# Order of ScalarE's and VectorE's operations in two attention loops, a later mask load, and an absolute value by masking bits

## The chip, the cores and the metric

The kernel runs on one core of one Trainium2 chip. The metric is device time in microseconds (us) of one execution; the median of three runs is compared. A core has TensorE (PE, matrix products and transposes), VectorE (DVE), ScalarE (ACT), GpSimd (POOL) and SyncE (SP, which here issues all transfers). Each runs its own list of instructions in order, and they meet at semaphores. Matrix products land in PSUM, in eight banks of 128 x 512 float32 (`ps[0]` to `ps[7]`), from which ACT or DVE read them.

## What is computed

Two transformer blocks over 512 tokens of width 1024, in float32. The first has window attention, a long convolution, differential attention, gates and a feed-forward network; the second has forgetting attention and stick-breaking attention (8 heads of 64 each), and a feed-forward network with a short convolution. The change touches two of the attentions:

```python
def diff_attention(q, k, v, lam):                      # first block, 4 heads
    s = einsum('bhcqd,bhckd->bhcqk', q, k) / sqrt(64)  # c = 0, 1
    p = softmax(s)
    a = p[:, :, 0] - lam * p[:, :, 1]
    return einsum('bhqk,bhkd->bhqd', a, v)

def stick_breaking_attention(q, k, v):                 # second block, 8 heads
    z = einsum('bhqd,bhkd->bhqk', q, k) * 64 ** -0.5
    log_beta = log_sigmoid(z)
    log_one_minus = where(mask, log_sigmoid(-z), 0.0)
    after = cumsum(log_one_minus, reverse=True) - log_one_minus
    weights = where(mask, exp(log_beta + after), 0.0)
    return einsum('bhqk,bhkd->bhqd', weights, v)
# the stick output then gets an rms norm over its 512 columns, gain sb_out_g
```

## The kernel before

**Weights.** All weight matrices pass through in 244 slots of at most 128 x 1024. SP loads a slot into one of three `wraw` buffers (line 2278), ACT rounds it to `whi` (L1562), DVE takes the rest `wlo` (L920), and PE multiplies three times (`hi*hi, hi*lo, lo*hi`) for each of the slot's four blocks; a block is six matmuls of 512 columns. ACT and DVE prepare a slot when PE starts the second slot ahead of it. The slots make groups, named after their weights (`sk`, `sv`, `fq`, `fk`, `fv`, ...), and a group's results are read at its last slot (L1450 reads those of `fq` and `fk`, L1187 those of `bA`).

**Attention beside the weights.** Each attention is a generator on every engine, with steps `u = 0, 1, 2, ...`; after a block of weights a group takes a step of it, 1, 2, 3 or 4 to a slot as the group's rate says. So the order on every engine is fixed by where the calls stand in the code. All engines take the same steps at the same blocks, each as far as its waits allow.

**Differential attention**, beside the groups `bA0` to `gC1`. Unit `u` is a query block and a head. PE: `scores(u)` into banks 4 and 5 (it waits until ACT has read them, semaphore `c_ex`), `turn(u - 2)` transposes the combined weights into bank 6 (waits for `c_cb`), `values(u - 3)`. DVE: `highest(u)` takes the maxima of banks 4 and 5 (L1210, L1212), then `combine(u - 1)` subtracts the two softmaxes (L1219 to L1225). ACT: `shares(u)`, the two exponentials (L1739). Every fourth unit the output is normed and turned through bank 6 as well; ACT takes `ochi` (L1756) and DVE `oclo` (L1244) from it, which frees the bank.

**Stick-breaking attention**, beside the groups `sv` (rate 1), `fq` (2), `fk` and `fv` (4). Units 0 to 7 have 512 columns of keys, 8 to 15 have 128, 16 to 23 have 384, 24 to 31 have 256. In step `u`:

- PE: `turn(u - 4)` transposes the sums `Lb` into bank 6, for even `u` `scores(u)` into banks 4 and 5 for two units, `values(u - 5)`.
- ACT: `copy(u)` reads the scores into `zb` (L1872), `logs(u - 1)` makes `log(1 + exp(-|z|))` (L1877, L1879), `weights(u - 4)` reads the turned bank 6 through an exponential (L1887).
- DVE: `sums(u - 2)` is the scan (L1375) and an addition (L1378), `parts(u)` makes `|z|` (L1367) and `min(-z, 0)` (L1368) from `zb`.

The norm of the stick output goes through the last quarter of the same bank 6, one quarter of 128 columns in each of four steps: PE turns it ahead of `turn`, ACT rounds it to `ohi` (L1864), DVE takes the rest `olo` (L1343). PE's next turn, quarter or not, waits until bank 6 has been read: by `weights` (semaphore `s_ev`) and, if there was a quarter, by `olo` (`o_lo`).

**The mask.** `mk` holds the masks of the second block's attentions. SP loads it behind the weights of slot 145, once POOL has finished a norm (`p_acc` at 35), and DVE copies it to `mkR` behind group `sq`, whose slots are 142 to 145.

Of the kernel before, what the change touches and what calls it, by code (L numbers as in the profile page):

```python
# [4 lines left out]

F32 = mybir.dt.float32
F32R = mybir.dt.float32r
ALU = mybir.AluOpType
ACT = mybir.ActivationFunctionType
AX = mybir.AxisListType  # L10
# [152 lines left out]
def build(nc, d, out):  # L163
# [231 lines left out]
    def tensor_program(t):  # L395
# [326 lines left out]
        def out_norm_piece(q, k):  # L722

            w.wait_ge(o_sc, 3 * q + 3)
            across(6, 3, W5[5][:, k * 128:(k + 1) * 128]).then_inc(o_tr, 1)
            return o_lo, 4 * q + k + 1

        def stick():
            w.wait_ge(qk_c, 8)

            def scores(u):

                n, wd = s_units[u][0], 128 * (s_units[u][0] + 1)
                for i in range(2):
                    take(4 + i)
                    base, j = 64 * i, s_units[u][1] // 2
                    mm(ps[4 + i][:, 0:wd], sqT[base:base + 64, j, n * 128:(n + 1) * 128], skT[base:base + 64, j, 0:wd], True, False)
                w.wait_ge(s_mk, 2)
                for i in range(2):
                    mm(ps[4 + i][:, n * 128:wd], identR[:], mkR[:], False, True).then_inc(s_qk, 1)  # L740
                    free[4 + i] = [(s_z, u + i + 1)]

            def turn(u):
                wd = 128 * (s_units[u][0] + 1)
                w.wait_ge(s_sum, u + 1)
                take(6)
                read = [(s_ev, u + 1)]
                if u >= 11 and u % 8 in (3, 4, 5, 6):
                    read.append(out_norm_piece(u // 8 - 1, u % 8 - 3))
                for k in range(wd // 128):  # L750
                    op = across(6, k, Lb[u % 5][:, k * 128:(k + 1) * 128])
                op.then_inc(s_tr, 1)
                free[6] = read

            def values(u):
                n, h = s_units[u]
                w.wait_ge(s_ev, u + 1)
                w.wait_ge(sv_c, n + 1)
                if h == 0:
                    take(7)  # L760
                for k in range(n + 1):
                    op = mm(ps[7][:, h * 64:(h + 1) * 64], PT2[u % 2][:, k * 128:(k + 1) * 128], sv[:, k, h * 64:(h + 1) * 64],
                            k == 0, k == n)
                op.then_inc(s_pv, 1)
                if h == 7:
                    free[7] = [(o_c, u // 8 + 1)]

            for u in range(37):
                if 4 <= u < 36:
                    turn(u - 4)  # L770
                if u < 32 and u % 2 == 0:
                    scores(u)
                if u >= 5:
                    values(u - 5)
                yield
# [135 lines left out]
    def vector_program(v):  # L911
# [290 lines left out]
        def differential():  # L1202
# [43 lines left out]
                                       ALU.subtract).then_inc(oc_lo, 1)  # L1246

            for u in range(22):
                if u < 16:
                    highest(u)  # L1250
                if 1 <= u <= 16:
                    combine(u - 1)
                if u >= 9 and u % 4 == 1:
                    low((u - 9) // 4)
                if u >= 7 and u % 4 == 3:
                    squares((u - 7) // 4)
                if 3 <= u < 19 and (u - 3) % 4 == 3:
                    scaled_out((u - 3) // 4)
                yield
# [100 lines left out]
        def stick():  # L1360
            def parts(u):
                wd = 128 * (s_units[u][0] + 1)
                z, L, nr = zb[u % 3], Lb[u % 5], W5[u % 3]
                w.wait_ge(s_z, u + 1)
                if u >= 5:
                    w.wait_ge(s_tr, u - 4)
                v.scalar_tensor_tensor(L[:, 0:wd], z[:, 0:wd], -1.0, z[:, 0:wd], ALU.mult, ALU.max).then_inc(s_ab, 1)  # L1367
                v.tensor_scalar(nr[:, 0:wd], z[:, 0:wd], -1.0, 0.0, ALU.mult, ALU.min).then_inc(s_ab, 1)  # L1368

            def sums(u):  # L1370
# [9 lines left out]
            for u in range(37):  # L1380
                if 2 <= u < 34:
                    sums(u - 2)
                if u < 32:
                    parts(u)
                if 15 <= u < 35 and u % 8 in (7, 0, 1, 2):
                    out_norm_piece((u - 15) // 8, (u - 15) % 8)
                yield

        fox_go = []
# [161 lines left out]
    def scalar_program(a):  # L1551
# [314 lines left out]
        def stick():  # L1866
# [20 lines left out]
                a.activation(PT2[u % 2][:, 0:wd], ps[6][:, 0:wd], ACT.Exp).then_inc(s_ev, 1)  # L1887

            for u in range(37):
                if u < 32:  # L1890
                    copy(u)
                if 1 <= u <= 32:
                    logs(u - 1)
                if 4 <= u < 36:
                    weights(u - 4)
                if 15 <= u < 35 and u % 8 in (7, 0, 1, 2):
                    out_norm_piece((u - 15) // 8, (u - 15) % 8)
                if u >= 5 and (u - 5) % 8 == 7:
                    q = (u - 5) // 8
                    w.wait_ge(s_pv, u - 4)  # L1900
# [369 lines left out]
    def sync_program(s):  # L2270
# [32 lines left out]
        weights(24, 66)  # L2303
        w.wait_ge(c_qk, 32)
        s.dma_start(x[:], x_dram).then_inc(in_res, 16)
        weights(66, 146)
        w.wait_ge(p_acc, 35)
        s.dma_start(mk[:], d["mask2"]).then_inc(in_mask, 16)
        weights(146, 158)
        w.wait_ge(fl_v, 5)  # L2310
        s.dma_start(f_dram, W5[5][0:8, :]).then_inc(fl_d, 16)
        w.wait_ge(fl_d, 16)
# [166 lines left out]
```

## Time and profile before

| | us |
|---|---|
| median of 3 runs (lowest, highest) | 1635.25 (1634.95, 1635.26) |
| the profiled execution, its time | 1634.98 |
| its span, first to last instruction | 1633.2 |
| PE busy | 1610.7, 99% of the span |
| DVE busy | 885.2, 54% |
| ACT busy | 636.1, 39% |
| POOL busy | 238.5, 15% |
| mean granted clock of PE | 0.999 |

Times in the trace count from the start of the span. The differential attention lies at about 442 to 533 us, the stick-breaking attention at about 1037 to 1162 us. PE's rows overlap: a matmul of 512 columns is drawn 0.39 us long, and the next starts 0.23 us after it, so PE can stand still for 0.16 us before a row shows a gap.

### The profile page before, as it was taken

What the parts mean: (1) busy time and instruction counts of PE and PEld (TensorE: products, weight loads), DVE (VectorE), ACT (ScalarE), POOL (GpSimd) and SP (SyncE); (2) the same over time, 40 slices, a digit from 0 to 9 for tenths busy, and PEclk for the clock granted to TensorE, in tenths of its full rate; (3) what the DMA queues carried; (4) which work ended last, traced back from release to release, by engine and by line L of the source; (5) the groups of instructions that cost most, each with busy time, mean ns of one, the idle gap of its engine ahead of it and who ended that gap; (6) DMA issues with size and microseconds to landing.
All of it is one profiled execution on the core that took longest, in us unless ns stands there. A gap on an engine that the chain in (4) does not pass through costs nothing.

```text
span 1633.2 us, 19219 instructions
## 1 busy us (share of the span) xinstructions
PE 1610.7 (99%) x7584; PEld 1275.3 (78%) x7584; DVE 885.2 (54%) x1447; ACT 636.1 (39%) x1089; POOL 238.5 (15%) x216
## 2 busy tenths in 40 slices
PE   7999999999999999999999999999999999999998
PEld 5667788876767888888888888786788888888887
DVE  6556456755477455433333324578555677777322
ACT  4332124456445433322322222456563344434222
POOL 1323303400031134111000203000013200000000
PEclk9999999999999999999999999999999999999999
DMA  7121113221111333233323322421103332322322
GB/s 276 42 77 40 52 57 104 90 78 52 66 52 59 122 92 95 89 99 103 99 95 99 96 90 73 168 65 39 53 3 102 92 101 87 95 91 90 129 91 77
DMA packets 39733, 142.12 MB, mean 87 GB/s; under 512 B 4531, under 2 KB 5299, under 8 KB 39260
## 3 DMA queue, kind: packets, MB, share of 16 engines
q1 hardware_dynamic: 39644, 140.89, 26.7%
q8 instruction: 60, 0.98, 0.3%
q14 instruction: 29, 0.24, 0.0%
HBM read 138.76 MB, written 2.11 MB: 86 GB/s over the span
## 4 chain that ended last, share of the span: by engine, by line
PE 91%; POOL 3%; DVE 2%; ACT 1%; issue 1%; DMA 0%; SPq 0%; POOLq 0%; ACTq 0%; DVEq 0%
PE ps L406 87%; PE ps L409 3%; POOL sqs L2151 2%; POOL sqt L2149 1%; DVE wlo L920 0%; ACT whi L1562 0%; DMA x<-in_x 0%; PE ps L906 0%; ACT PT L1887 0%; ACT zb L1872 0%; DVE W L1375 0%; ACT Lb L1877 0%; DVE tp L1120 0%; ACT tp L1685 0%; DVE st L1107 0%
## 5 line engine op out<-in xcount | busy, mean ns | idle before, releaser
L920 DVE TENSOR_TENSOR wlo<-wraw,whi 128x1024 fp32r<-128x1024 f32 (+2 forms) x244 | 304.2, 1251 | 448.9 <-ACT whi L1562 448.4
L406 PE MATMUL ps<-hThi,whi 128*128 128x512 f32 x1128 | 455.9, 404 | 0.0
L1562 ACT ACTIVATE whi<-wraw 128x1024 fp32r<-128x1024 f32 (+2 forms) x244 | 252.1, 1037 | 484.5 <-PE ps L406 454.6
L406 PE MATMUL ps<-hThi,wlo 128*128 128x512 f32 x1128 | 440.4, 390 | 0.0
L406 PE MATMUL ps<-hTlo,whi 128*128 128x512 f32 x1128 | 440.0, 390 | 0.0
L406 PEld LDWEIGHTS ps<-hThi,whi 128*128 128x128 f32 x1128 | 212.3, 188 | 59.7 <-issue 19.1
L406 PEld LDWEIGHTS ps<-hThi,wlo 128*128 128x128 f32 x1128 | 212.1, 188 | 45.5
L406 PEld LDWEIGHTS ps<-hTlo,whi 128*128 128x128 f32 x1128 | 212.5, 188 | 44.5 <-issue 3.6
L406 PE MATMUL ps<-whi,hThi 128*128 128x512 f32 (+1 forms) x224 | 87.0, 388 | 0.4 <-ACT rk L1679 0.4
L406 PE MATMUL ps<-whi,hTlo 128*128 128x512 f32 (+1 forms) x224 | 84.2, 376 | 0.0
L406 PE MATMUL ps<-wlo,hThi 128*128 128x512 f32 (+1 forms) x224 | 83.9, 375 | 0.0
L406 PE MATMUL ps<-whi,achi 128*128 128x512 f32 x176 | 69.2, 393 | 0.0
L406 PE MATMUL ps<-whi,aclo 128*128 128x512 f32 x176 | 68.6, 390 | 0.0
L406 PE MATMUL ps<-wlo,achi 128*128 128x512 f32 x176 | 68.5, 389 | 0.0
L406 PE MATMUL ps<-achi,whi 128*128 128x512 f32 x176 | 68.5, 389 | 0.0
L406 PE MATMUL ps<-aclo,whi 128*128 128x512 f32 x176 | 68.5, 389 | 0.0
L406 PE MATMUL ps<-achi,wlo 128*128 128x512 f32 x176 | 68.5, 389 | 0.0
L2168 POOL TENSOR_TENSOR ft<-ft,R 128x512 f32<-128x512 f32 x22 | 27.9, 1290 | 199.1 <-ACT ft L1806 199.1
L1817 ACT ACTIVATE ft<-vt,vec 128x512 f32<-128x512 f32 x44 | 34.8, 813 | 51.1 <-DVE vt L1312 51.1
L2265 POOL TENSOR_TENSOR small<-small,vec 128x1 f32<-128x1 f32 x4 | 2.2, 541 | 349.1 <-DVE small L1537 349.1
L406 PEld LDWEIGHTS ps<-whi,hThi 128*128 128x128 f32 x224 | 42.2, 189 | 10.4 <-issue 2.9
L406 PEld LDWEIGHTS ps<-whi,hTlo 128*128 128x128 f32 x224 | 42.2, 188 | 7.9
(310 smaller groups left out, 2429.8 us busy)
## 6 DMA issues: line engine op xcount, KB each, us to landing
wraw<-in_ws SPq DMA_DIRECT2D x236, 512.0 KB, 3.5
x<-in_x SPq DMA_DIRECT2D x4, 512.0 KB, 5.7
x<-in_x SPq DMA_DIRECT2D x1, 2048.0 KB, 9.9
Fb<-forget_rows SPq DMA_DIRECT2D x1, 2048.0 KB, 8.5
out<-ys SPq DMA_DIRECT2D x8, 256.0 KB, 2.4
w<-in_w SPq DMA_DIRECT2D x2, 512.0 KB, 12.3
dec<-in_dec SPq DMA_DIRECT2D x1, 1024.0 KB, 14.9
wraw<-in_ws SPq DMA_DIRECT2D x4, 256.0 KB, 2.6
```

Of the source, the lines that this page charges most:

```text
L406: return t.matmul(o, l, r, start=first, stop=last)
L409: return t.transpose(ps[b][:, c * 128:(c + 1) * 128], src, ident)
L920: v.tensor_tensor(wlo[h][:, 0:width(i)], wraw[h][:, 0:width(i)], whi[h][:, 0:width(i)].bitcast(F32), ALU.subtract).then_inc(lo_done[h], 1)
L1562: a.activation(whi[h][:, 0:width(i)], wraw[h][:, 0:width(i)], ACT.Copy).then_inc(hi_done[h], 1)
L1817: a.activation(ft[i][:], vt[q % 4][:], ACT.Identity, bias=col("cb2", c), scale=col("cw2", 88 + c)).then_inc(v_a, 1)
L2149: g.tensor_tensor(sqt[:], xT[:, f, :], xT[:, f, :], ALU.mult).then_inc(p_acc, 1)
L2151: g.tensor_tensor(sqs[:], sqs[:], sqt[:], ALU.add).then_inc(p_acc, 1)
L2168: g.tensor_tensor(t[:], t[:], R1[:], ALU.mult).then_inc(u_sr, 1)
L2265: g.tensor_tensor(small[:, 8 + b:9 + b], small[:, 4 + b:5 + b], col("mhalf"), ALU.pow).then_inc(w_r, 1)
```

## The change

Five edits. No instruction is added or taken away except that one operation on DVE is exchanged for another.

1. Differential attention, DVE: `combine(u - 1)` is issued before `highest(u)`.
2. Stick-breaking attention, ACT: `weights(u - 4)` first, then the quarter, then `copy(u)` and `logs(u - 1)`.
3. Stick-breaking attention, DVE: the quarter after the sums and before `parts(u)`. The quarters run one step later on all three engines (steps 16 to 19, 24 to 27 and 32 to 35; before 15 to 18, 23 to 26, 31 to 34).
4. `|z|` is made by clearing the sign bit of an integer view, a `tensor_scalar`, in place of a `scalar_tensor_tensor` that takes `max(-z, z)`.
5. SP loads the mask behind slot 148 in place of slot 145.

```diff
@@ PE, stick, turn(u)
-                if u >= 11 and u % 8 in (3, 4, 5, 6):
-                    read.append(out_norm_piece(u // 8 - 1, u % 8 - 3))
+                if u >= 12 and u % 8 > 3:
+                    read.append(out_norm_piece(u // 8 - 1, u % 8 - 4))
@@ DVE, differential
             for u in range(22):
+                if 1 <= u <= 16:
+                    combine(u - 1)
                 if u < 16:
                     highest(u)
-                if 1 <= u <= 16:
-                    combine(u - 1)
@@ DVE, stick, parts(u)
-                v.scalar_tensor_tensor(L[:, 0:wd], z[:, 0:wd], -1.0, z[:, 0:wd], ALU.mult, ALU.max).then_inc(s_ab, 1)
+                v.tensor_scalar(L[:, 0:wd].bitcast(I32), z[:, 0:wd].bitcast(I32), 0x7FFFFFFF, None, ALU.bitwise_and).then_inc(s_ab, 1)
@@ DVE, stick
                 if 2 <= u < 34:
                     sums(u - 2)
+                if 16 <= u < 36 and u % 8 < 4:
+                    out_norm_piece(u // 8 - 2, u % 8)
                 if u < 32:
                     parts(u)
-                if 15 <= u < 35 and u % 8 in (7, 0, 1, 2):
-                    out_norm_piece((u - 15) // 8, (u - 15) % 8)
@@ ACT, stick
             for u in range(37):
+                if 4 <= u < 36:
+                    weights(u - 4)
+                if 16 <= u < 36 and u % 8 < 4:
+                    out_norm_piece(u // 8 - 2, u % 8)
                 if u < 32:
                     copy(u)
                 if 1 <= u <= 32:
                     logs(u - 1)
-                if 4 <= u < 36:
-                    weights(u - 4)
-                if 15 <= u < 35 and u % 8 in (7, 0, 1, 2):
-                    out_norm_piece((u - 15) // 8, (u - 15) % 8)
@@ SP
-        weights(66, 146)
+        weights(66, 149)
         w.wait_ge(p_acc, 35)
         s.dma_start(mk[:], d["mask2"]).then_inc(in_mask, 16)
-        weights(146, 158)
+        weights(149, 158)
```

The order of VectorE's instructions in steps 2 and 3 of the differential attention before (the two gate operations stand at the head of each step, `Pc_142` is unit 1):

```order
L1187 SCALAR_TENSOR_TENSOR gate_109<-gate_109,ps 128x512 x2
L1210 TENSOR_REDUCE st<-ps 128x1
L1212 TENSOR_SCALAR st<-st 128x1
L1210 TENSOR_REDUCE st<-ps 128x1
L1212 TENSOR_SCALAR st<-st 128x1
L1219 RECIPROCAL st<-st 128x1
L1221 SCALAR_TENSOR_TENSOR st<-st,small 128x1
L1223 RECIPROCAL st<-st 128x1
L1225 SCALAR_TENSOR_TENSOR Pc_142<-Pc_143,st,Pc_142 128x512
```

The same step of VectorE after the change (its lines are numbered one higher):

```order
L1188 SCALAR_TENSOR_TENSOR gate_109<-gate_109,ps 128x512 x2
L1220 RECIPROCAL st<-st 128x1
L1222 SCALAR_TENSOR_TENSOR st<-st,small 128x1
L1224 RECIPROCAL st<-st 128x1
L1226 SCALAR_TENSOR_TENSOR Pc_142<-Pc_143,st,Pc_142 128x512
L1211 TENSOR_REDUCE st<-ps 128x1
L1213 TENSOR_SCALAR st<-st 128x1
```

The combination of unit 1 has moved ahead of the maxima of unit 2.

ScalarE's instructions in stick steps 23 and 24 before, around the rounding of a weight slot (`zb_207` is the copy of unit 23, `PT_1_195` the turned bank of unit 19, `ohi` the quarter):

```order
L1872 ACTIVATE zb_207<-ps 128x384
L1877 ACTIVATE Lb_202<-Lb_202 128x384
L1879 ACTIVATE Lb_202<-Lb_202,vec 128x384
L1887 ACTIVATE PT_1_195<-ps 128x384
L1864 ACTIVATE ohi<-ps,vec 128x128
L1562 ACTIVATE whi_56<-wraw_53 128x1024
L1872 ACTIVATE zb_205<-ps 128x256
L1877 ACTIVATE Lb_203<-Lb_203 128x384
L1879 ACTIVATE Lb_203<-Lb_203,vec 128x384
L1887 ACTIVATE PT_0_194<-ps 128x384
```

The same place on ScalarE after the change:

```order
L1888 ACTIVATE PT_1_195<-ps 128x384
L1873 ACTIVATE zb_207<-ps 128x384
L1878 ACTIVATE Lb_202<-Lb_202 128x384
L1880 ACTIVATE Lb_202<-Lb_202,vec 128x384
L1563 ACTIVATE whi_56<-wraw_53 128x1024
L1888 ACTIVATE PT_0_194<-ps 128x384
L1865 ACTIVATE ohi<-ps,vec 128x128
L1873 ACTIVATE zb_205<-ps 128x256
```

The reading of the turned bank now heads each step, the quarter has gone from step 23 to step 24, and the slot's rounding keeps its place at the step's end.

VectorE in the same stretch before, from the first sum of step 24 on (`Kf` reads a result of group `fk`, `olo` is a quarter):

```order
L920 TENSOR_TENSOR wlo_59<-wraw_53,whi_56 128x1024
L1450 SCALAR_TENSOR_TENSOR Kf<-ps,R_160 128x512
L1375 SCALAR_TENSOR_TENSOR W_1_189<-W_1_189,Lb_202 128x384
L1378 TENSOR_TENSOR Lb_202<-zb_206,W_1_189 128x384
L1367 SCALAR_TENSOR_TENSOR Lb_204<-zb_205 128x256
L1368 TENSOR_SCALAR W_0_188<-zb_205 128x256
L1343 SCALAR_TENSOR_TENSOR olo<-ps,vec,ohi 128x128
```

And VectorE there after the change:

```order
L921 TENSOR_TENSOR wlo_59<-wraw_53,whi_56 128x1024
L1451 SCALAR_TENSOR_TENSOR Kf<-ps,R_160 128x512
L1376 SCALAR_TENSOR_TENSOR W_1_189<-W_1_189,Lb_202 128x384
L1379 TENSOR_TENSOR Lb_202<-zb_206,W_1_189 128x384
L1344 SCALAR_TENSOR_TENSOR olo<-ps,vec,ohi 128x128
L1368 TENSOR_SCALAR Lb_204<-zb_205 128x256
L1369 TENSOR_SCALAR W_0_188<-zb_205 128x256
```

The quarter is two operations nearer to the head of the step, but still behind the slot's rest, the reading of `Kf` and the sums; the absolute value has become a `TENSOR_SCALAR`.

## Rows read from the trace of the kernel before

**Rows 1.** Waits of PE: engine, line and tile, waited for, total us, times, longest.

```profile
PE ps L409 <- DVE olo L1343: 3.0, 6, 0.9
PE ps L409 <- DVE Pc L1225: 1.5, 1, 1.5
...
PE ps L409 <- ACT PT L1887: 0.7, 2, 0.3
```

**Rows 2.** Timeline, 452 to 457 us: start, length, engine, line, operation, [idle before].

```profile
452.82 0.68 DVE L1210 TENSOR_REDUCE st<-ps 128x1 f32<-128x512 f32 x1
...
453.73 0.69 ACT L1739 ACTIVATE Pc<-ps,st 128x512 f32<-128x512 f32 x1 [1.49 <-DVE st L1212]
...
454.39 0.15 DVE L1219 RECIPROCAL st<-st 128x1 f32<-128x1 f32 x1
...
455.04 0.75 DVE L1225 SCALAR_TENSOR_TENSOR Pc<-Pc,st,Pc 128x512 f32<-128x512 f32 x1
...
455.85 0.65 PE L409 MATMUL ps<-vec,Pc 128*128 128x128 f32 x4 [1.48 <-DVE Pc L1225]
456.43 1.13 PE L406 MATMUL ps<-kcT,qcT 64*128 64x512 f32 x4
```

**Rows 3.** Timeline, 492 to 494 us, where a normed output frees bank 6.

```profile
492.73 0.75 DVE L1244 SCALAR_TENSOR_TENSOR oclo<-ps,vec,ochi 128x512 fp32r<-128x512 f32 x1 [0.24 <-ACT ochi L1756]
...
493.69 0.49 PE L409 MATMUL ps<-vec,Pc 128*128 128x128 f32 x3
```

**Rows 4.** Timeline, 1105 to 1108 us, stick steps 16 and 17.

```profile
1105.14 0.49 ACT L1872 ACTIVATE zb<-ps 128x384 f32<-128x384 f32 x1 [1.45 <-PE ps L406]
...
1106.26 0.39 PE L406 MATMUL ps<-hTlo,whi 128*128 128x512 f32 x1
...
1106.49 0.39 PE L406 MATMUL ps<-hThi,wlo 128*128 128x512 f32 x1
...
1106.72 0.35 DVE L1343 SCALAR_TENSOR_TENSOR olo<-ps,vec,ohi 128x128 fp32r<-128x128 f32 x1 [0.23 <-ACT ohi L1864]
...
1107.22 0.30 PE L409 MATMUL ps<-vec,W 128*128 128x128 f32 x1 [0.34 <-DVE olo L1343]
```

**Rows 5.** Timeline, 1125 to 1133 us, stick steps 23 to 25.

```profile
1125.14 0.48 ACT L1872 ACTIVATE zb<-ps 128x384 f32<-128x384 f32 x1
...
1125.47 0.49 PE L409 MATMUL ps<-vec,Lb 128*128 128x128 f32 x3
...
1126.95 0.36 ACT L1864 ACTIVATE ohi<-ps,vec 128x128 fp32r<-128x128 f32 x1
...
1127.20 1.06 ACT L1562 ACTIVATE whi<-wraw 128x1024 fp32r<-128x1024 f32 x1
...
1132.03 0.35 DVE L1343 SCALAR_TENSOR_TENSOR olo<-ps,vec,ohi 128x128 fp32r<-128x128 f32 x1
...
1132.52 0.30 PE L409 MATMUL ps<-vec,W 128*128 128x128 f32 x1 [0.94 <-DVE olo L1343]
```

**Rows 6.** Timeline, 1150 to 1156 us, stick steps 31 to 33.

```profile
1150.05 0.37 ACT L1872 ACTIVATE zb<-ps 128x256 f32<-128x256 f32 x1
...
1150.56 0.38 PE L409 MATMUL ps<-vec,Lb 128*128 128x128 f32 x2
...
1155.47 0.30 PE L409 MATMUL ps<-vec,W 128*128 128x128 f32 x1 [0.52 <-DVE olo L1343]
```

**Rows 7.** VectorE's groups by form, 1000 to 1170 us: count, busy us, mean ns, idle before.

```profile
L1367 DVE SCALAR_TENSOR_TENSOR Lb<-zb 128x384 f32<-128x384 f32 x8 | 4.4, 555 | 1.6 <-ACT zb L1872 1.6
...
L1368 DVE TENSOR_SCALAR W<-zb 128x384 f32<-128x384 f32 x8 | 2.8, 353 | 0.0
```

**Rows 8.** The mask's tile: duration ns min/median/max, first and last start us.

```profile
L2308 SPq DMA_DIRECT2D mk<-in_mask x1: 328/328/328, 995.0 to 995.0; - x1
L1509 DVE CAST mkR<-mk x1: 219/219/219, 1006.0 to 1006.0; 128x128 fp32r<-128x128 f32 x1
...
DMA to landing us min/median/max: 2.9/2.9/2.9
```

More of the change, by code:

```diff
@@ L7 @@
 F32R = mybir.dt.float32r
+I32 = mybir.dt.int32
 ALU = mybir.AluOpType
```

## The prediction

> **What bounds the kernel now.** PE is busy for 99% of the span, so I read first what it waits for. Most of the list lies at the start of the program or in norms that the change doesn't touch. Three entries lie in the two attentions: `olo` 3.0 us in 6 waits, `PT` (`weights`) 0.7 us in 2, and `Pc` (`combine`) 1.5 us in one [rows 1]. The reader should see what is not in the list: PE never waits for the sums `Lb` of the stick attention, only for its bank 6 to be read.
>
> A gap in a row is shorter than what PE loses. Two matmuls start 0.23 us apart (1106.26, 1106.49), but each is drawn 0.39 us long [rows 4]. So 0.16 us is to be added to each gap: the turn at 1107.22 was due at 1106.72 and lost 0.50 us, where its row says 0.34. In this measure the eight stick waits cost 3.7 + 8 x 0.16 = 5.0 us, the differential one 1.48 + 0.16 = 1.64 us. The change can win 6.6 us, 0.4% of 1635, and no more.
>
> **The change, part by part.**
>
> *Differential, removed.* PE's turn of unit 1 starts at 455.85 and was due at 454.21. DVE comes to this step at 452.82, and does the maxima of unit 2 first; the combination runs from 454.39 to 455.79, 1.40 us [rows 2]. In the new order the combination runs from 452.82 to 454.22, and the turn starts at 454.28. That wins 1.57 us.
>
> *Differential, what is late next.* The maxima of unit 2 now start at 454.14, 1.32 us later. ACT's first exponential starts 0.91 us after them (452.82 to 453.73) [rows 2], so at 455.05, and is done with its sum some 0.77 us later, at 455.82; the second ends at 456.6. Behind the turn on PE stands `scores(3)`, which needs banks 4 and 5. It follows the turn by 0.58 us (455.85 to 456.43), so it is due at 454.86, waits until 455.87 for bank 4, and its second half until 456.67 for bank 5. It ends at 457.2; before, at 456.43 + 1.06 = 457.49. Of 1.57 us 0.3 is left. Six steps on, the maxima still come some 0.3 us late, as DVE meets a weight slot first and then does the combination ahead of them, and behind them stands the normed output: `oclo` ends at 493.48 and PE turns at 493.69, 0.21 us later, of which some 0.15 is the way from DVE to PE (1107.07 to 1107.22) [rows 3, 4]. This loses 0.2. Sum: 0.1 us won.
>
> *Stick, a wait that goes.* At step 16 ACT stands idle for 1.45 us before `copy(16)` at 1105.14, for scores that PE makes behind its turn, and reads the turned bank only after that. With `weights` first, the reading and the quarter's `ohi` (0.36 us) [rows 5] fit into the idle time. DVE's `olo` at 1106.72 stood idle for its `ohi` [rows 4], and now also has the two `parts` operations behind it (0.555 + 0.353 us) [rows 7]: it starts at 1105.8, is done at 1106.2, and PE's turn, due at 1106.72, doesn't wait. The 0.50 us go. Of the eight waits the two large ones below (1.10 and 0.68) are left to tell; the five others have 5.0 - 0.50 - 1.78 = 2.7 us. I moved the rows in the same way through those steps, each operation to the later of its engine and its input: two were waits for `weights` behind two logarithms, which it now leads, and go; the three others go where DVE is through with its sums in time. I am left with 0.3 us in two of them, where DVE isn't; 2.4 us go.
>
> *Stick, two waits that stay.* At step 25 PE waits until 1132.52, 0.94 + 0.16 = 1.10 us, for an `olo` that starts at 1132.03 [rows 5]. In front of it DVE has a slot's rest `wlo`, one `Kf` and the sums, and `wlo` begins when ACT's `whi` is done. That begins later now: before, ACT did `copy(23)` at 1125.14 without waiting for the turn of step 23, and reached `whi` 2.06 us later, with `weights` and a quarter (0.25 us, 1126.95 to 1127.20) between. Now step 23 opens with a wait for the turn, which ends at 1125.47 + 0.49 = 1125.96; the same operations without the quarter are 1.81 us, and `whi` begins at 1127.8, 0.6 us later. DVE has the two `parts` less in front of `olo`, 0.91 us at 384 columns [rows 7] and about two thirds of it at the 256 here, so 0.6. The two cancel, and the wait stays at 1.1 us. At step 33 the pattern returns: the turn of step 31 ends at 1150.94, `copy(31)` had begun at 1150.05 [rows 6], and now comes after the turn and 0.27 us of `weights`, at 1151.2. Without the quarter `whi` is 0.65 late; here DVE had no `parts` to put behind `olo` (steps 32 and on have none), so the whole 0.65 reaches PE: 0.52 + 0.16 becomes 1.3 us.
>
> *Sum for the stick attention:* 5.0 before; left are 0.3 + 1.1 + 1.3 = 2.7. Won 2.3, between 0 (all waits come back behind slots) and 5.0 (none does).
>
> *The absolute value.* The trace shows no integer operation on DVE. Bounds are the same tile's two forms at 384 columns: 555 ns as it is, 353 ns as the `TENSOR_SCALAR` beside it [rows 7]. I take 353, as it is the nearest in form. DVE then has 0.2 us a step less, 5 us over 32 units, but all of it behind `olo`, and PE waits for no sum. At either end it is worth 0; a way for it to lose would be a form slower than 555, which the same argument hides.
>
> A page speaks against this edit: the Trainium skill, "SBUF — State Buffer" (Who interferes with whom), has a VectorE operation at its two-port double rate and a GpSimd operation block each other for their whole length. No run here shows it; GpSimd has three operations per norm in this stage, the last of which is needed for a quarter that now comes a step later than before, so by that rule the sum would stay as it is. By the Trainium skill, "VectorE: DVE Perf Modes" (What auto-detection actually checks), the double rate is open to one source in SBUF as far as the firmware enables it for the operation; by that the new form is at either bound, and the sum the same.
>
> *The mask.* SP's load goes out at 995.0 and lands 2.9 us later; DVE copies it at 1006.0 [rows 8]. The load still waits for the same norm, and slots 146 to 148 go out ahead of it instead of standing behind. Lost only if it came 8 us later; PE shows no wait here, so nothing is won either. 0 us; the cover is those 8 us.
>
> **Sum.** 0.1 + 2.3 = 2.4 us. The profiled execution took 1634.98 us with a span of 1633.2, 0.27 us below the median; from the median, 1635.25 - 2.4 = 1632.9, or 0.14%. A measurement of this kernel can tell 0.2%, 3.3 us, from no change.
>
> **The rivals.**
>
> *A. As above, the waits move behind the slots.* 1631.9 to 1634.2. Chance 0.54.
>
> *B. The gain comes whole.* The bank is read right behind the turn, and DVE reaches `olo` in time also at slots: 5.0 us in the stick attention, 0 to 1.6 in the other, 1630.2 down to 1628.6. It needs `whi` at steps 23 and 31 no later than before. For it: 8 of 8 stick waits are of the kind that the new order aims at. Against it: at 1132.03 `olo` has no idle time in its row, so its `ohi` was there, and DVE itself was late [rows 5]. With partial forms (one of the two waits gone) everything below 1632.0: chance 0.25.
>
> *C. Nothing is won.* A second wait of the kind of the one for bank 4 (1.0 us) stands at a later gate step of the differential attention, and in the stick attention two more slot starts have their `whi` 0.65 us late. 2.4 - 1.0 - 1.3 leaves 0.1 us: 1635.2, with 1634.2 to 1636.5 around it. For it: DVE meets a slot's rest or gates ahead of the combination in every second step. Against it: at those steps the second exponential ends, by the same reckoning, before its bank is due. Chance 0.17.
>
> *D. Slower.* ACT is in order, and each odd step's `copy`, which needed no new scores, now stands behind the turn: 1.2 us later at steps 23 and 31. If the sums were due that tightly, PE would wait 1.2 us at each of the ten odd steps from 13 to 31: 12 us, less the 5.0, gives 1642. It decides from the point where a sum is ready less than 1.2 us ahead of its turn. Against it: no wait for a sum in the list [rows 1]. Chance 0.04.
>
> **How the numbers follow.** The likeliest is A, 1632.9. From 1630.2 to 1636.0 takes in most of B's whole stick gain and nearly all of C, leaving out D and B's end with both gains, some 0.15. A alone has 1631.9 to 1634.2. Faster by over 0.2% is below 1631.98: B, and a little of A's edge, 0.27. Slower by over 0.2% is above 1638.5: D and a rest, 0.05. Within: 0.68.
>
> **What would show it.** In the new trace PE should have no wait for `Pc`, but one of some 1 us for ACT's reading of banks 4 and 5 ahead of `scores(3)`, near 455. The `olo` waits should be fewer, the two large ones near 1130 and 1153, each with a `wlo` just before its `olo`; no `PT` wait. The new absolute value should show 353 ns at 384 columns. The forecast is wrong if either of those two waits is under 0.5 us, if a wait for `Lb` appears, or if `whi` of step 23 starts no later against its turn than before.

## The result, and the profile after

The changed kernel takes 1639.88 us (median of 15 runs) against 1635.25 us before (15 runs). The ratio of the means, 1.0024 with a 95% interval of 1.0017 to 1.0030, says 0.24% slower, where 1632.9 us had been forecast. One execution of each kernel here, two of e10 and one of e11 were over 10% longer than the others; ranges and ratios leave them out, medians count them. The profiled execution took 1639.91 us with a span of 1638.1, 4.9 us more than before.

I laid each PE instruction of one trace beside the same one of the other and read how much later it starts. This shift is -0.4 us at 450 us. Between 455 and 489 us it grows by 7.4, to 7.0 us. It stays there to 1100, past the mask's place, and falls by 2.2 to 2.4 us in the stick attention. So the forecast failed in the differential attention alone.

PE's waits, to be laid beside [rows 1] (lines are numbered one higher now):

```profile
PE ps L410 <- DVE olo L1344: 2.3, 2, 1.2
PE ps L407 <- ACT Pc L1740: 1.9, 3, 0.9
PE ps L410 <- DVE Pc L1226: 1.2, 1, 1.2
```

The wait for `Pc` was to go and is still there. The waits for ScalarE's reading of banks 4 and 5 (`ACT Pc`) are three, not one. Only the two for `olo` are as forecast. The timeline at the first gate step answers to [rows 2]:

```profile
452.08 2.53 POOL L2118 TENSOR_TENSOR merged<-merged,gate 128x512 f32<-128x512 f32 x2 [134.25 <-DVE gate L1188]
...
452.51 0.16 DVE L1220 RECIPROCAL st<-st 128x1 f32<-128x1 f32 x1
...
452.70 0.69 DVE L1222 SCALAR_TENSOR_TENSOR st<-st,small 128x1 f32<-128x1 f32 x1
...
453.31 0.15 DVE L1224 RECIPROCAL st<-st 128x1 f32<-128x1 f32 x1
...
453.50 1.66 DVE L1226 SCALAR_TENSOR_TENSOR Pc<-Pc,st,Pc 128x512 f32<-128x512 f32 x1
...
455.21 0.66 PE L410 MATMUL ps<-vec,Pc 128*128 128x128 f32 x4 [1.15 <-DVE Pc L1226]
...
456.81 2.07 PE L407 MATMUL ps<-kcT,qcT 64*128 64x512 f32 x3 [0.94 <-ACT Pc L1740]
```

Two operations of the combination are longer: L1222 takes 0.69 us and L1226 1.66, where a step without a gate shows 0.22 and 0.75:

```profile
465.17 0.22 DVE L1222 SCALAR_TENSOR_TENSOR st<-st,small 128x1 f32<-128x1 f32 x1
...
465.50 0.75 DVE L1226 SCALAR_TENSOR_TENSOR Pc<-Pc,st,Pc 128x512 f32<-128x512 f32 x1
```

The combination lasts from 452.51 to 455.16, 2.65 us and not 1.40. The GpSimd row is the one to look at: it adds the branch to `merged`, two additions back to back until 454.61. L1222 ends when the first addition does (452.08 + 1.26 = 453.34, by half of the row), and L1226 ends 0.55 us after the second. GpSimd isn't slowed, 2.53 us for two as before. In the trace of before these additions ran from 452.39 to 454.92, beside the maxima, which showed their usual 0.68 [rows 2], and reached only the first of the combination's two operations:

```profile
452.39 2.53 POOL L2117 TENSOR_TENSOR merged<-merged,gate 128x512 f32<-128x512 f32 x2 [134.26 <-DVE gate L1187]
...
454.58 0.34 DVE L1221 SCALAR_TENSOR_TENSOR st<-st,small 128x1 f32<-128x1 f32 x1
```

In the changed kernel the next three combinations at gate steps read the same: 0.66 and 1.65 us at 458.06 and 458.82, 0.67 and 1.67 at 478.14 and 478.91, 0.66 and 1.66 at 484.06 and 484.83, each with two additions beside them.

PE's granted clock, in windows over the same place (columns: window, its length, busy us and number of instructions of PE, of its weight loads, DVE, ACT and POOL, the granted clock, then DMA):

```profile
440.00:455.00 15.00, 14.06 (x60) 8.80 (x58) 10.38 (x20) 5.13 (x11) 2.53 (x2) 1.00 0.23 70
455.00:460.00 5.00, 3.85 (x10) 1.82 (x11) 4.86 (x11) 2.05 (x5) 2.49 (x2) 0.65 0.00 0
460.00:465.00 5.00, 5.00 (x20) 4.31 (x20) 3.14 (x7) 2.50 (x5) 0.00 (x0) 0.67 0.00 0
465.00:500.00 35.00, 34.04 (x171) 23.88 (x170) 25.94 (x58) 15.79 (x35) 8.31 (x8) 1.00 0.16 46
```

PE lost 1.31 us in the first wait and 1.01 in the second, which ends at 456.81. The clock falls to the lower level of 1.2 GHz within the second wait, at 456.5, and is back at 2.4 at 463.3. Before, it stood at 1.00 through this stage. In these 6.8 us matmuls start 0.43 us apart:

```profile
461.89 0.63 PE L407 MATMUL ps<-oalo,whi 128*128 128x512 f32 x1
462.32 0.63 PE L407 MATMUL ps<-oahi,wlo 128*128 128x512 f32 x1
462.75 0.63 PE L407 MATMUL ps<-oahi,whi 128*128 128x512 f32 x1
```

By their mean granted clocks not every execution has the fall. Nine of the fourteen of ordinary length have 0.997 or 0.998 and took 1639.1 to 1641.5 us. The other five have 0.999 or 1.0 and took 1636.4 to 1638.2, still more than any of the kernel before (1634.3 to 1636.1).

Three later steps wait for scores, at 482.24, 488.36 and 494.80, since their maxima came late:

```profile
482.24 1.91 PE L407 MATMUL ps<-kcT,qcT 64*128 64x512 f32 x4 [0.50 <-ACT Pc L1740]
488.36 1.69 PE L407 MATMUL ps<-kcT,qcT 64*128 64x512 f32 x4
494.80 1.91 PE L407 MATMUL ps<-kcT,qcT 64*128 64x512 f32 x4 [0.46 <-ACT Pc L1740]
```

Four score matmuls undisturbed take 1.13 us [rows 2]. The shift grows by 3.2 us over these three places. The first two stand behind the combinations of the gate steps at 478 and 484. The third stands behind one without additions of gates. There GpSimd multiplies `ocs` for the norm, and L1222 stands beside it in the same way:

```profile
491.19 1.09 DVE L1222 SCALAR_TENSOR_TENSOR st<-st,small 128x1 f32<-128x1 f32 x1
...
491.23 1.04 POOL L2130 TENSOR_TENSOR ocs<-ocs,st 128x512 f32<-128x512 f32 x1
```

Before, that multiplication lay beside the maxima (485.17 to 486.21), and L1221 took 0.22.

The stick attention answers to [rows 5, 6]. At step 25:

```profile
1133.68 1.23 DVE L921 TENSOR_TENSOR wlo<-wraw,whi 128x1024 fp32r<-128x1024 f32 x1 [1.38 <-ACT whi L1563]
...
1134.83 0.69 DVE L1451 SCALAR_TENSOR_TENSOR Kf<-ps,R 128x512 f32<-128x512 f32 x1
...
1135.43 0.95 DVE L1376 TENSOR_TENSOR_SCAN W<-W,Lb 128x384 f32<-128x384 f32 x1
1136.41 0.56 DVE L1379 TENSOR_TENSOR Lb<-zb,W 128x384 f32<-128x384 f32 x1
1136.89 0.35 DVE L1344 SCALAR_TENSOR_TENSOR olo<-ps,vec,ohi 128x128 fp32r<-128x128 f32 x1
...
1137.38 0.30 PE L410 MATMUL ps<-vec,W 128*128 128x128 f32 x1 [1.05 <-DVE olo L1344]
```

`olo` stands behind the slot's rest, `Kf` and the sums, and PE loses 1.21 us (0.16 more than its row says, as before); at step 33, near 1160, it loses 1.37. Of the other six of eight waits four are gone, two are down to 0.2 us. ScalarE's `whi` of step 23 starts 2.37 us after the step's turn, where it was 1.73 before: 0.6 later, as forecast. The new absolute value takes what the operation beside it takes [rows 7]:

```profile
L1368 DVE TENSOR_SCALAR Lb<-zb 128x384 int32<-128x384 int32 x8 | 2.8, 354 | 0.3 <-ACT zb L1873 0.2
L1369 DVE TENSOR_SCALAR W<-zb 128x384 f32<-128x384 f32 x8 | 2.8, 353 | 0.0
```

### The profile page after: what moved, and what is told of

The parts are those of the page before. It is cut to its first block, busy times and chain, and to the rows that moved or that the text cites. A ratio compares the mean times of both kernels' runs of the same rounds, so it can differ in the third digit from the quotient of the medians.

```text
span 1638.1 us, 19219 instructions
## 1 busy us (share of the span) xinstructions
PE 1615.5 (99%) x7584; PEld 1278.8 (78%) x7584; DVE 887.2 (54%) x1447; ACT 638.2 (39%) x1089; POOL 240.3 (15%) x216
## 4 chain that ended last, share of the span: by engine, by line
PE 90%; POOL 3%; DVE 3%; ACT 1%; issue 1%; DMA 0%; SPq 0%; POOLq 0%; ACTq 0%; DVEq 0%
PE ps L407 87%; PE ps L410 3%; POOL sqs L2152 2%; POOL sqt L2150 1%; ACT whi L1563 0%; DVE wlo L921 0%; DVE Pc L1226 0%; ACT Pc L1740 0%; DVE st L1211 0%; DMA x<-in_x 0%; DVE gate L1188 0%; PE ps L907 0%; DVE st L1222 0%; POOL small L2044 0%; DVE tp L1121 0%
```

## The experiments

There were three rounds of timing, each beside the kernel before on the same chip, and a last one of single profiles. The rounds' medians of the kernel before differ by 0.5 us, so each row is to be read against its own. The theory, P: VectorE's operations that read SBUF twice stand still while GpSimd adds, this makes the combination 1.25 us longer at gate steps, and from it come the waits and the fall of the clock. The rival, Q: the new order of VectorE's queue does it by itself.

| kernel | us, median (lowest to highest) | before | ratio, 95% |
|---|---|---|---|
| e1 stick edits, no differential edit | 1632.44 (1631.42 to 1632.96) | 1635.39 | 0.9981 (0.9973 to 0.9990) |
| e2 differential edit alone | 1642.99 (1639.96 to 1643.76) | 1635.39 | 1.0041 (1.0028 to 1.0053) |
| e3 as e2, additions of one column | 1635.25 (1634.88 to 1636.41) | 1635.39 | 1.0000 (0.9992 to 1.0009) |
| e4 before, additions of one column | 1634.90 (1633.72 to 1636.67) | 1635.39 | 0.9999 (0.9990 to 1.0008) |
| e5 as e1, quarter ahead of the sums | 1630.19 (1629.09 to 1631.54) | 1634.93 | 0.9968 (0.9956 to 0.9980) |
| e6 stick order alone | 1632.85 (1632.53 to 1635.03) | 1634.93 | 0.9989 (0.9980 to 0.9998) |
| e7 old order, late additions | 1642.57 (1642.03 to 1643.56) | 1634.93 | 1.0048 (1.0036 to 1.0061) |
| e8 new order, late additions | 1633.41 (1632.36 to 1635.74) | 1634.93 | 0.9991 (0.9982 to 1.0000) |
| e9 as e5, combination in the middle | 1629.76 (1628.99 to 1630.31) | 1635.06 | 0.9968 (0.9955 to 0.9980) |
| e10 changed, first additions late | 1637.79 (1635.46 to 1639.36) | 1635.06 | 1.0014 (1.0004 to 1.0023) |
| e11 changed, one tensor input | 1638.80 (1635.04 to 1640.73) | 1635.06 | 1.0017 (1.0008 to 1.0026) |
| e12 stick order on ScalarE alone | 1634.69 (1633.83 to 1635.11) | 1635.06 | 0.9998 (0.9989 to 1.0007) |

**e1.** The edit, in the changed kernel:

```diff
             for u in range(22):
-                if 1 <= u <= 16:
-                    combine(u - 1)
                 if u < 16:
                     highest(u)
+                if 1 <= u <= 16:
+                    combine(u - 1)
```

> The changed kernel with one edit undone: in the differential attention VectorE does highest(u) ahead of combine(u - 1) again. Theory P (the combination beside GpSimd's gate additions is what failed; the other edits did as forecast): the trace shows the stick attention's loss of PE time down by 2.2 us (7.02 to 4.81 in the shift of the changed kernel), and nothing lost elsewhere, so 1635.25 - 2.2 = 1633.0 us, between 1632.6 and 1633.5, and the granted clock of PE never falls near 456 us. Rival R (part of the 7 us comes from the other edits, the mask's or the quarters', which only shows together): 1634 or more.

Measured: 1632.44, 0.2 under the range. The shift against before falls by 2.2 us in the stick attention, and there is no other loss. This is as P has it.

**e2.** The same lines changed the other way, in the kernel before.

> The kernel before with one edit: combine(u - 1) ahead of highest(u) in the differential attention. Theory P: everything that was lost comes from here, 7.4 us of which some 3.5 is PE's granted clock falling to half for 6.8 us, so 1642.4 us with the fall and 1638.5 to 1640 without it; VectorE's L1221 and L1225 show 0.69 and 1.66 us at the four gate steps in place of 0.22 and 0.75. Rival R: under 1637, the rest of the loss needs the other edits.

Measured: 1642.99. The five executions are of two kinds: 1639.96 and 1640.73 with a mean granted clock of 0.999, and 1642.99 to 1643.76 with 0.997. The profiled one, which shows no fall of the clock, is of the first kind, and its shift grows by 5.15 us in the differential attention, against 7.4 in the changed kernel's trace with the fall. Its waits:

```profile
PE ps L406 <- ACT Pc L1739: 1.9, 3, 0.9
PE ps L409 <- DVE Pc L1225: 1.2, 1, 1.2
```

They are the same as in the changed kernel. So the fall costs 2.3 us in the traces, 2.8 between the two kinds (1640.35 to 1643.14, their medians) and 3.2 between those of the changed kernel (1636.78 to 1639.94). It comes in some executions and not in others, at the same waits. Why stays open.

**e3 and e4.** On GpSimd:

```diff
+                if j == 1:
+                    m, gt = m[:, 0:1], gt[:, 0:1]
                 g.tensor_tensor(m, m, gt, ALU.add).then_inc(b_p, 1)
```

> As the one before, but GpSimd's eight additions merged + gate of the second branch (those that lie in the first steps of the differential attention) are done over one column of 512, the rest is left out; the order of all engines and every semaphore stay. Theory P (VectorE's two operations with two inputs in SBUF stand while GpSimd reads SBUF): L1221 and L1225 show 0.22 and 0.75 us at all four gate steps, the combination takes 1.40 us, PE's turn(1) doesn't wait, scores(3) waits about 1.0 us, the four later steps have their maxima 1.25 us earlier and wait under 0.2 us each, the clock stays at full speed: within 1 us of the kernel before, 1634.9 to 1636.2. Rival Q (the order of VectorE's queue alone does it, the additions are no matter): as the one before, within 0.5 us.

> The kernel before with the same eight additions cut to one column (the rest of the sum is left out), as a control. In the old order only L1221 lies beside GpSimd's additions, at steps 2 and 6: 0.34 should become 0.22 and the wait of turn(1) 0.1 us shorter. Both theories: within 0.3 us of the kernel before.

Both kernels leave out the rest of the sum. Measured: 1635.25 and 1634.90, not to be told from the kernel before (e4 is 0.5 us below it, where 0.3 at most was expected). In e4 the turn waits 1.52 us in place of 1.64, as expected. In e3 the combination of the first gate step is short again, with the order of e2:

```profile
451.82 0.15 DVE L1219 RECIPROCAL st<-st 128x1 f32<-128x1 f32 x1
452.01 0.22 DVE L1221 SCALAR_TENSOR_TENSOR st<-st,small 128x1 f32<-128x1 f32 x1
452.15 0.16 DVE L1223 RECIPROCAL st<-st 128x1 f32<-128x1 f32 x1
452.34 0.75 DVE L1225 SCALAR_TENSOR_TENSOR Pc<-Pc,st,Pc 128x512 f32<-128x512 f32 x1
```

The only wait left in the list from the differential attention is the one forecast for `scores(3)`:

```profile
PE ps L406 <- ACT Pc L1739: 0.9, 1, 0.9
```

The shift of e3 grows by 0.55 us over the stage, and 4.6 of the 5.15 us of e2 come with the additions. Q is out. Of the 0.55 us, 0.1 is lost at the first gate step. The rest goes at one place, where bank 5 is read late, and ahead of it stands GpSimd's multiplication of `ocs`, which this edit does not touch:

```profile
483.67 1.09 DVE L1221 SCALAR_TENSOR_TENSOR st<-st,small 128x1 f32<-128x1 f32 x1
483.70 1.04 POOL L2131 TENSOR_TENSOR ocs<-ocs,st 128x512 f32<-128x512 f32 x1
...
487.56 1.62 PE L406 MATMUL ps<-kcT,qcT 64*128 64x512 f32 x4
```

L1221 is 0.87 us longer there than elsewhere, and the four matmuls 0.49 longer than undisturbed. So the order by itself may cost 0.1 us only; no run moves the multiplication away. The cut additions also make GpSimd's work shorter, which is why two tests with whole additions follow.

**e7.** The converse: the old order, with GpSimd's additions moved beside the combination.

```diff
+                if j == 1 and k % 2 == 0:
+                    w.wait_ge(c_mx, (12, 16, 28, 32)[k // 2])
                 g.tensor_tensor(m, m, gt, ALU.add).then_inc(b_p, 1)
```

> The converse test: the order of before everywhere, but GpSimd's gate additions of the four gate steps wait until the maxima of that step are done, so that they lie beside the combination, which stands behind the maxima. Nothing is left out. Theory P (two-input operations of VectorE stand while GpSimd adds): L1221 and L1225 take 0.7 to 1.1 and 1.66 us at these four steps, the combination ends 1.3 to 1.8 us later, PE's turn(1) waits 2.9 to 3.4 us in place of 1.63, turns 2, 5 and 6 wait 0.6 to 1.2 us each; the sum is 3.7 to 5.5 us over the kernel before, and some 3.4 more in executions in which PE's clock falls: 1639 to 1644. Rival Q (the place of the maxima matters, not the additions): nothing on VectorE changes, 1635.3 within 0.5.

Measured: 1642.57, 7.6 us slower, with VectorE's and PE's order untouched.

```profile
453.94 1.32 DVE L1221 SCALAR_TENSOR_TENSOR st<-st,small 128x1 f32<-128x1 f32 x1
...
453.98 2.48 POOL L2119 TENSOR_TENSOR merged<-merged,gate 128x512 f32<-128x512 f32 x2 [136.49 <-DVE st L1212]
...
455.37 1.64 DVE L1225 SCALAR_TENSOR_TENSOR Pc<-Pc,st,Pc 128x512 f32<-128x512 f32 x1
...
457.07 1.11 PE L409 MATMUL ps<-vec,Pc 128*128 128x128 f32 x4 [3.34 <-DVE Pc L1225]
```

The combination now ends at 457.0, and PE's wait is 3.34 + 0.16 = 3.5 us, a little over the range. Turn 2 had no wait of its own; turns 5 and 6 had 1.7 and 1.3, more than the 0.6 to 1.2 expected. The clock fell in this trace too (0.61 granted from 455 to 460 us), at 455.9, within the long wait. P's mechanism holds, and the time is in its range; its single waits were put somewhat low.

**e8.** The changed kernel, with the additions waiting for the combination (`c_cb` at 8, 12, 24, 28 in place of `c_mx`).

> The changed kernel, in which GpSimd's gate additions wait until the step's combination is done, so that they lie beside the maxima, whose inputs are in PSUM. Nothing is left out. Theory P: combinations of 1.40 us, turn(1) without a wait, scores(3) waits 1.0 us for ScalarE's reading of banks 4 and 5 and the clock stays at full speed; the differential attention costs as much as before (as with additions of one column), the stick attention wins its 2.2: 1632.4 us, within 0.6. Rival U (additions beside the maxima, or beside the next gate operation, hold up VectorE as well): 1634 to 1640.

Measured: 1633.41, with everything computed, against 1639.88 for the changed kernel in another round. That is 0.4 over P's range and 0.6 under U's. In the trace the differential attention costs 0.6 us more than before, where P had nothing, with L1222 at 1.09 us beside the `ocs` multiplication as in e3, and the stick attention wins its 2.2. GpSimd's additions (454.04 to 456.54) lie beside the maxima and the next gate operations, and neither is longer:

```profile
454.60 0.68 DVE L1211 TENSOR_REDUCE st<-ps 128x1 f32<-128x512 f32 x1
...
455.40 1.28 DVE L1188 SCALAR_TENSOR_TENSOR gate<-gate,ps 128x512 f32<-128x512 f32 x2
```

The gate operation has two inputs as well, but one of them in PSUM.

**e11.** What in the operation makes it stand? In the changed kernel:

```diff
-                v.scalar_tensor_tensor(P0[:], P1[:], st[:, o + 4:o + 5], P0[:], ALU.mult, ALU.add).then_inc(c_cb, 1)
+                v.tensor_scalar(P0[:], P1[:], st[:, o + 4:o + 5], None, ALU.mult).then_inc(c_cb, 1)
```

> The changed kernel, with the last operation of the combination cut to one tensor input: Pc[1] times the factor, without the addition of Pc[0] (that sum is left out). GpSimd's additions stay beside it. If only VectorE's operations with two tensors in SBUF stand, this one takes what such an operation takes elsewhere, 0.42 us for 512 columns, at all four gate steps, while L1222 keeps its 0.67; the combination ends 1.2 us earlier, and the time is 1634.5 to 1636.5. If any read of SBUF by VectorE stands beside GpSimd's additions, it takes 1.2 to 1.6 us there, and 0.42 at the undisturbed steps, and the time is 1638 to 1641.

Measured: 1638.80, and at a gate step and at one without gates:

```profile
453.09 1.40 DVE L1226 TENSOR_SCALAR Pc<-Pc,st 128x512 f32<-128x512 f32 x1
...
464.56 0.49 DVE L1226 TENSOR_SCALAR Pc<-Pc,st 128x512 f32<-128x512 f32 x1
```

The rows decide for the second alternative: this operation with one tensor input takes 1.39 to 1.41 us at all four gate steps and 0.49 elsewhere, so two inputs are not what it needs to stand. The time by itself would not tell: of nine executions five have the lower clock of 0.997 and took 1638.5 to 1640.7, four have 0.999 or 1.0 and took 1635.0 to 1636.6. The time of a `TENSOR_SCALAR` grows by 0.52 ns for each column (L1369 of the changed kernel: 221 ns at 128 columns, 420 at 512), that of the two-input `TENSOR_TENSOR` L1379 by 1.04 (293 and 692 ns). So it reads about two columns in a nanosecond, and it stands all the same. The Trainium skill, "SBUF — State Buffer" (Who interferes with whom), names both kinds: a VectorE instruction with two inputs in SBUF against a GpSimd one that reads SBUF, and one at its two-port double rate; whichever comes second is blocked for the other's whole length, and `tensor_reduce` is free of it. The traces agree. Beside GpSimd's additions an operation with two inputs takes 1.66 us (the changed kernel) and 1.64 (e7), one with a single input at the faster rate 1.40 (e11), and `TENSOR_REDUCE` its usual 0.68 (e8). Away from them the first takes 0.75 (e3, e8) and the second 0.49.

**e10.** Only the first pair of additions waits (`if j == 1 and k == 0: w.wait_ge(c_cb, 8)`).

> The changed kernel, in which only the first two of GpSimd's gate additions (first gate step) wait for the combination; at the other three gate steps they lie beside it as in the changed kernel. It parts the first contention and the fall of PE's clock from the later waits. Theory: turn(1) doesn't wait, scores(3) waits 1.0 us, the clock doesn't fall in any execution, and so 3 us go as well; the later waits of scores at steps 6 to 9 stay, 2.5 to 3.3 us. So between the kernel with all additions late (1633.41) and the changed one (1639.88): 1635.9 to 1636.9, with no execution over 1638. Rival: the clock falls all the same behind the waits of 478 to 495 us, in some executions, and these are 3 us longer.

Measured: 1637.79, over the range. The profiled execution has 1635.66, no wait of a turn for `Pc`, a shift that grows by 4.1 us over the stage, and a clock of 1.00 all along. But of its nine comparable executions two stand at 1639.28 and 1639.36, and four show a clock of 0.998. The part "no execution over 1638" failed. Whether it was by the rival's fall of the clock, no trace shows.

Three more profiles were to show where the clock falls then:

> The kernel with the first two additions late once more, for one profile. Of its nine comparable executions four stood at 1635.5 to 1636.4 with a granted clock of 0.999 to 1.0 and five at 1637.4 to 1639.4 with 0.998 or 0.999; the profiled one had no fall. Theory: where the clock falls, it falls right behind a wait of scores near 480, 486 or 492 us, and matmuls start 0.43 us apart for some microseconds. Rival: it falls elsewhere, in a place that has nothing to do with these waits.

> The same kernel and the same expectation, for a second profile, since the fall comes in about half of its executions.

> The same kernel and the same expectation, for a third profile.

Measured: 1636.07, 1636.51 and 1637.79, with clocks of 1.0, 0.999 and 1.0. In none of them did it fall in the attentions, nor anywhere else before the last 4 us. Where it falls in the slower executions of e10, if it does, stays open. The three also differ by 1.7 us in their times. That difference arises at the very start: PE's first matmul waits for `x` until 8.31, 7.60 and 9.49 us, and at 20 us the shifts against the kernel before are -0.8, -0.5 and 1.0. Executions of this kernel differ by such an amount without any fall.

**e6.** The new order of the stick attention without the new absolute value and the later mask.

> Only the new order in the stick attention, on ScalarE, VectorE and TensorE: no new absolute value, no later mask, the old order in the differential attention. By the forecast the absolute value and the mask are worth 0: same as the kernel with them, 1632.4, within 0.4 us. Rival: the 0.2 us a step less on VectorE (0.553 to 0.354 us at 384 columns) matter at the two slot steps where VectorE is late, up to 0.4 us each, so 1632.8 to 1633.3.

Measured: 1632.85. Against its own kernel before it wins 2.1 us, where e1 won 2.9, but the two intervals overlap, and by time alone the rival is not out. The traces say more: the shift falls by 2.1 us here and 2.2 in e1, and the two large waits are 1.20 and 1.38 us here and 1.20 and 1.36 in e1. Absolute value and mask are worth 0.1 us there, not to be told from nothing.

**e12.** As e1, with VectorE's quarter behind `parts(u)`, as it was before.

> The kernel with the differential order undone (1632.44), with VectorE's quarter behind parts(u) as before and the quarters at the new steps: the new order of the stick attention on ScalarE alone. It parts the 2.2 to 2.5 us won between the two engines. By the reckoning in the prediction, olo comes 0.55 to 0.9 us later wherever there are parts ahead of it: the wait at step 25 grows from 1.20 to 1.8 us, the one at step 33 stays 1.37, step 16 and the like have 0.5 us to spare: 1633.0 to 1634.0. Rival: VectorE's move is worth nothing, 1632.4, or all of it, 1634.9.

Measured: 1634.69, and a shift of -0.75 at 1102 us and -0.74 at 1155. ScalarE's order alone wins nothing; the rival "all of it" is right. VectorE's move alone was not run. The two large waits are 1.60 and 1.37 us, where 1.8 and 1.37 were expected, but new ones come at steps that were thought to have time, as here, where `olo` was ready in every respect but VectorE's queue:

```profile
1113.32 0.35 DVE L1368 TENSOR_SCALAR Lb<-zb 128x384 int32<-128x384 int32 x1
1113.59 0.35 DVE L1369 TENSOR_SCALAR W<-zb 128x384 f32<-128x384 f32 x1
1113.86 0.34 DVE L1344 SCALAR_TENSOR_TENSOR olo<-ps,vec,ohi 128x128 fp32r<-128x128 f32 x1
...
1114.35 0.52 PE L410 MATMUL ps<-vec,Lb 128*128 128x128 f32 x3 [0.56 <-DVE olo L1344]
```

**e5.** As e1, with the quarter moved once more:

```diff
-                if 2 <= u < 34:
-                    sums(u - 2)
                 if 16 <= u < 36 and u % 8 < 4:
                     out_norm_piece(u // 8 - 2, u % 8)
+                if 2 <= u < 34:
+                    sums(u - 2)
```

> The kernel with the differential order undone (1632.44 us) and one more move: in the stick attention VectorE does the quarter's olo ahead of the sums, not behind them. It tests what the two waits that stay are made of. In that kernel PE waits 1.20 us at 1130.58 and 1.37 us at 1153.44, each for an olo which had its ohi long before (1127.2 and 1150.9) and stood behind a slot's rest, a Kf and the sums (1.46 and 1.06 us). Theory S (VectorE's queue, not ScalarE, is what is late there): olo starts at 1128.3 and 1151.6, both waits go, 2.5 us won, 1629.9 us, and at most 1631.0 if the later sums make a new wait. Rival T (the quarter at steps that begin no slot now holds up the sums, since VectorE waits for ohi there: up to 1.1 us at each of 8 such steps): a wait for Lb or PT appears and the time is 1632.4 or more.

Measured: 1630.19. No `olo`, `PT` or `Lb` is left among PE's waits, and the shift falls by 4.8 us in the stage, of the 5.0 that its waits cost before. `olo` follows `Kf` now:

```profile
1128.96 0.69 DVE L1451 SCALAR_TENSOR_TENSOR Kf<-ps,R 128x512 f32<-128x512 f32 x1
1129.56 0.34 DVE L1344 SCALAR_TENSOR_TENSOR olo<-ps,vec,ohi 128x128 fp32r<-128x128 f32 x1
```

**e9.** As e5, and at step 2 of the differential attention alone `highest(2, (0,))`, `combine(1)`, `highest(2, (1,))`, with the first additions late.

> The fastest kernel so far (quarter ahead of the sums, 1630.19 us) with the one wait of the differential attention that it has left: at step 2 alone VectorE does the maximum of bank 4, then the combination, then the maximum of bank 5, and GpSimd's additions of that step wait for the combination. Reckoned from the rows of the kernel before: the combination runs from 453.61 to 455.01, PE's turn waits 0.85 us in place of 1.63; bank 5 is read out at 456.7 and was due at 456.15, a new wait of 0.5. Won 0.3 us, 1629.9, not to be told from 1630.2 by time, only in the trace. Rival: both waits are longer, since the first exponential is also late, and it is 0.5 slower; or the second wait doesn't come and 0.8 are won.

Measured: 1629.76, 0.4 under e5 and not to be told from it. PE's turn waits 0.56 + 0.16 = 0.72 us; then bank 5 is late by as much as was won, and the shift is 0.1 higher behind the stage than ahead of it. The stage's 1.6 us were not to be had in any of the three places that were tried for the combination. e5 and e9 are the fastest versions, 0.32% below the kernel before.

## Why the prediction was wrong

**The step that failed** is the first: "In the new order the combination runs from 452.82 to 454.22". The 1.40 us were read where the combination stood before, behind the maxima. In its new place it stands beside GpSimd's additions and takes 2.65 us, shown by e3 and e8 (short again, in two ways, in the same order) and e7 (long in the old order). The turn still waited for 1.31 of 1.64 us. A trace of an old position doesn't show which of an operation's neighbours it will have in the new one; the row was there to be seen, GpSimd's two additions from 452.39 on in the trace of before, and the 0.34 us of L1221 at 454.58, where steps without gates have 0.22. The prediction weighed the rule of the Trainium skill, "SBUF — State Buffer" (Who interferes with whom), against the absolute value, where it changed nothing, and not against the edit that moved two-input operations next to GpSimd.

**What is late next** had the right mechanism and was mis-sized. The wait for bank 4 came (1.01 us, as forecast), and a second of 0.78 for bank 5 (e2's trace, 1.91 us for 1.13). But the loss "six steps on" was put at 0.2 us, and was 3.2, since three more steps had their maxima late: two by the longer combination of a gate step, the third by the lateness left over and by the `ocs` multiplication beside L1222. Without the gate additions it is 0.5 (e3, e8). That meets the first half of rival C's condition, three times over. The time itself lies above 1638.5, where the forecast had rival D and a rest, 0.05 in all.

**The clock** was in no part of the sum. It fell within the second of the two waits for 6.8 us, and costs 2.3 to 3.2 us in those executions that have it.

**The stick attention** was right: 2.3 won by forecast, 2.2 to 2.4 measured; the two large waits 1.1 and 1.3 by forecast, 1.21 and 1.37 measured; small ones 0.3 by forecast, 0.2 and 0.2 measured. Rival B, the whole gain, needed one more move (e5). Rival D didn't come: there is no wait for `Lb`. But the forecast gave ScalarE's order a share of the gain that it doesn't have alone (e12). What VectorE's move would win alone is not shown.

**The absolute value and the mask** were right: 354 ns at 384 columns where 353 was taken, and 0.1 us in the traces (e6).

The account of the loss, by the traces: order of the differential attention with what stays of the contention in e3 +0.6, contention with the gate additions +4.6, clock +2.3, stick attention -2.2 to -2.4, and -0.4 between the starts of the two executions: 4.7 to 4.9, for a difference of the spans of 4.9.

## What to carry to other kernels

Price an operation in the place that it moves to: list what GpSimd does in that stretch, and for each VectorE operation whether it reads SBUF twice, or fast, or from PSUM. Such operations are best put where GpSimd is idle, or GpSimd's behind them with a semaphore, which here turned 1639.9 us into 1633.4. When a wait stays after its input has long been ready, as `olo` did, look at the queue of the engine that serves it and move that one operation to the head: from e1 to e5 the stick attention's gain in the traces went from 2.2 to 4.8 us this way.

## What was not expected of the hardware

A `TENSOR_SCALAR` with a single tensor in SBUF stood for GpSimd's additions like one with two inputs (1.40 us for 0.49). A 128x1 operation with two inputs stood as long as the addition that was under way (up to 1.32 us for 0.22 in e7), while `RECIPROCAL` on 128x1, between them, kept its 0.15. With the same two waits of 1.3 and 1.0 us PE's clock kept its full speed in e2's trace and fell to half in the changed kernel's; of e2's five executions three have the lower mean clock that goes with a fall. In e7's trace it fell in a wait of 3.5 us, and not at the two later ones of 1.7 and 1.3.
